# Other places for the modulation units in the first block's weight ring

## What is computed

```python
mod = (c_act @ w_ada + b_ada)[:, None, :]
sh1, sc1, g1, sh2, sc2, g2 = jnp.split(mod, 6, axis=-1)
h = rmsnorm(x, norm1_w) * (1 + sc1) + sh1
u = h @ w_in                       # 1024 x 5632
...                                # pooling, short convolution, 8 attention heads
x = x + g1 * (merged @ w_out)
h2 = rmsnorm(x, norm2_w) * (1 + sc2) + sh2
x = x + g2 * ((jax.nn.silu(h2 @ w_gate) * (h2 @ w_up)) @ w_down)   # D_FF = 2816
```

## Time and profile before

| | us |
|---|---|
| median of 3 runs | 1804.53 (1804.48 to 1804.78) |
| the profiled execution | 1801.64 |
| its span, first to last instruction | 1799.8 |
| first block, first layer: product(0) to product(0) of the second | 51.4 to 509.2 |
| first block, second layer: to the end of product(65) | 509.2 to 928.2 |

### The profile page before, as it was taken

How to read it: one execution, slowest core, us unless ns; L and a number is a source line. 1 busy time by engine, 2 the same in 40 slices (tenths; PEclk the granted TensorE clock), 3 DMA queues, 4 the chain that set the end, 5 groups by cost and what they waited for, 6 DMA issues and landing times.

```text
span 1799.8 us, 18780 instructions
## 1 busy us (share of the span) xinstructions
PE 1572.9 (87%) x7463; PEld 1082.9 (60%) x7463; DVE 924.3 (51%) x1334; ACT 619.3 (34%) x877; POOL 49.8 (3%) x66
## 2 busy tenths in 40 slices
PE   2889987999979998799969995999996996799985
PEld 2667766878767776688858874333335875433331
DVE  4897576864479656654547765110006675311102
ACT  2335544343343454443425651111114572211111
POOL 2000000000000000000020200000000010000000
PEclk9999998999989999899989997999998988899998
DMA  9676445866568634474546324999994416599994
GB/s 341 219 273 215 141 140 173 302 215 210 176 223 282 200 137 151 153 233 146 214 125 204 129 90 192 384 409 409 409 388 150 157 48 241 197 409 409 409 409 190
DMA packets 149963, 427.65 MB, mean 238 GB/s; under 512 B 8104, under 2 KB 16544, under 8 KB 149872
## 3 DMA queue, kind: packets, MB, share of 16 engines
q1 hardware_dynamic: 146192, 417.43, 63.3%
q0 software_dynamic: 3456, 8.87, 1.8%
q10 hardware_dynamic: 224, 0.07, 0.0%
HBM read 425.30 MB, written 1.05 MB: 237 GB/s over the span
## 4 chain that ended last, share of the span: by engine, by line
PE 44%; DVE 6%; SPq 6%; DMA 3%; ACT 1%; issue 1%; DVEq 0%
PE gp L2080 12%; PE gp L2433 9%; PE gp L2252 8%; SPq L725 6%; PE gp L2452 4%; PE mp L2473 2%; DMA raw_more<-in_exp_w_up 2%; PE gp L2418 2%; PE mp L2307 1%; PE mp L2306 1%; PE mp L2271 1%; DVE stats L1623 1%; PE mp L2295 1%; PE mp L2315 1%; DMA raw<-in_w_in 1%
## 5 line engine op out<-in xcount | busy, mean ns | idle before, releaser
L1276 DVE TENSOR_TENSOR wlo<-raw,whi 128x2048 fp32r<-128x2048 f32 (+1 forms) x132 | 289.5, 2194 | 228.8 <-ACT whi L833 227.6
L833 ACT ACTIVATE whi<-raw 128x2048 fp32r<-128x2048 f32 (+1 forms) x132 | 242.2, 1835 | 368.0 <-PE gp L2080 215.7
L2080 PE MATMUL gp<-whi,xt_hi 128*128 128x512 f32 (+1 forms) x800 | 318.6, 398 | 32.1 <-DVE xt_lo L1325 14.1
L2080 PE MATMUL gp<-wlo,xt_hi 128*128 128x512 f32 (+1 forms) x800 | 312.1, 390 | 0.0
L2080 PE MATMUL gp<-whi,xt_lo 128*128 128x512 f32 (+1 forms) x800 | 311.5, 389 | 0.0
L2080 PEld LDWEIGHTS gp<-whi,xt_hi 128*128 128x128 f32 x800 | 154.8, 193 | 73.1 <-DVE wlo L1276 18.1
L2080 PEld LDWEIGHTS gp<-whi,xt_lo 128*128 128x128 f32 x800 | 154.9, 194 | 31.4
L2080 PEld LDWEIGHTS gp<-wlo,xt_hi 128*128 128x128 f32 x800 | 155.1, 194 | 29.1 <-issue 0.2
L1948 DVE TENSOR_SCALAR pr<-slots,key,dg 128x128 f32<-128x128 f32 x64 | 19.3, 344 | 260.5 <-PE gp L2463 260.5
L2252 PE MATMUL gp<-whi,xt_hi 128*128 128x512 f32 (+1 forms) x224 | 85.6, 382 | 6.3 <-DVE xt_lo L1668 3.1
L1186 DVE SCALAR_TENSOR_TENSOR acc<-raw,cact,acc 128x1024 f32<-128x1024 f32 x69 | 88.4, 1282 | 1.4
(11 more groups left out here) (392 smaller groups left out, 2324.6 us busy)
## 6 DMA issues: line engine op xcount, KB each, us to landing
raw<-in_w_in SPq DMA_DIRECT2D x60, 1024.0 KB, 5.9
raw<-in_w_ada SPq DMA_DIRECT2D x42, 1024.0 KB, 5.3
raw_deep<-in_exp_w_down SPq DMA_DIRECT2D x36, 1024.0 KB, 16.9
raw_deep<-in_exp_w_gate SPq DMA_DIRECT2D x30, 1024.0 KB, 14.3
raw_deep<-in_exp_w_up SPq DMA_DIRECT2D x30, 1024.0 KB, 16.7
raw<-in_w_gate SPq DMA_DIRECT2D x20, 1024.0 KB, 5.2
raw<-in_w_up SPq DMA_DIRECT2D x20, 1024.0 KB, 5.3
raw<-in_w_down SPq DMA_DIRECT2D x20, 1024.0 KB, 5.0
```

Source lines behind the costliest of these rows:

```text
L833: act.activation(slot(whi, s % SPLIT, units, cols), slot(raw, g % RAW, units, cols), ACT.Copy).then_inc(hi_done.sem, 1)
L1276: dve.tensor_tensor(slot(wlo, s % SPLIT, units, cols), slot(raw, g % RAW, units, cols), slot(whi, s % SPLIT, units, cols).bitcast(F32), AL ...
L2080: mm = pe.matmul(gp[:, q % 2, t, 0:wide], a[:, chunk, ts], w[:, unit, c0:c0 + wide], start=first and n == 0 and m == 0, stop=last and n == ...
```

## The change

The table that places the modulation units becomes three lists. Units 9 to 11 (vector 2) stand behind split units 2 to 4 as before. Units 12 to 19 (vectors 3 and 4), which stood behind 5 to 12, now stand behind 10, 12, 13, 15, 16, 17, 21 and 22. Units 20 to 31, which stood behind 13 and 32 to 42, stand behind every second unit from 32 to 54. The last stays behind 60.

With that the places of three sums move. TensorE's `sum_mod(3)` goes from behind product(9) to behind the heads, just ahead of `sum_mod(4)`, and VectorE's `take_mod(3)` with it. TensorE's `sum_mod(5)` goes from behind product(35) to behind product(43) and the turning of columns there, and VectorE's `take_mod(5)` from step 37 to step 45. Vectors 3 and 4 now share bank 0 of `mp`, in different columns.

```diff
-LATE = 2
-AFTER = {LATE + s: AHEAD + s for s in range(12)}
-AFTER.update({S_FF + LATE + i: AHEAD + 12 + i for i in range(6 * ADA - 1 - 12)})
-AFTER[S_DOWN + 6] = 6 * ADA + AHEAD - 1
+GATE_AT = (2, 3, 4)
+NORM_AT = (10, 12, 13, 15, 16, 17, 21, 22)
+FF_AT = tuple(S_FF + 2 + 2 * i for i in range(12))
+AFTER = {s: AHEAD + i for i, s in enumerate(GATE_AT + NORM_AT + FF_AT + (S_DOWN + 6,))}
...
-        MOD_BANK = (0, 1, 0, 2, 0, 2)
+        MOD_BANK = (0, 1, 0, 0, 0, 2)
+        MOD_COL = (0, 0, 0, 0, KD, 0)
...
                 for s in range(10):
-                    if s == 9:
-                        take_mod(3)
                     split(s + 2)
...
+                dve.wait_ge(*acc_read.at(l, 5))
+                take_mod(3)
                 take_mod(4)
                 norm_columns(1, 3)
...
-                    if s == S_FF + 7:
+                    if s == S_FF + 15:
                         take_mod(5)
...
-                sum_mod(3, l)
...
-                        pe.wait_ge(*mod_taken.at(l, 4))
+                        pe.wait_ge(*mod_taken.at(l, 3))
...
                 pe.wait_ge(*s_max.at(l, HEADS))
+                sum_mod(3, l)
                 sum_mod(4, l)
...
-                    if s == S_FF + 5:
-                        sum_mod(5, l)
                     if r == 1 and j >= 1:
-                        if j == 2:
+                        if j == 4:
                             pe.wait_ge(*mod_taken.at(l, 6))
                         turn_ab(j - 1)
+                    if s == S_FF + 13:
+                        pe.wait_ge(*ft_lo.at(l, X_ACT + 4))
+                        sum_mod(5, l)
```

More of the change, by code:

```diff
@@ L71 @@
 AHEAD = 2 * ADA + 1
[L72 to L76 removed]
+GATE_AT = (2, 3, 4)
+NORM_AT = (10, 12, 13, 15, 16, 17, 21, 22)
+FF_AT = tuple(S_FF + 2 + 2 * i for i in range(12))
+AFTER = {s: AHEAD + i for i, s in enumerate(GATE_AT + NORM_AT + FF_AT + (S_DOWN + 6,))}
+assert AHEAD % RAW == 0 and max(AFTER) == S_DOWN + 6 and len(AFTER) == 6 * ADA and max(FF_AT) == S_DOWN
 def ring_order():
@@ L1295, in take_mod @@
                     else:
-                        src = gp[:, 0, vec, 0:KD] if l == 0 and vec < 2 else mp[:, MOD_BANK[vec], 0:KD]
+                        c = MOD_COL[vec]
+                        src = gp[:, 0, vec, 0:KD] if l == 0 and vec < 2 else mp[:, MOD_BANK[vec], c:c + KD]
                         dve.tensor_tensor(modc[:, vec, :], src, pcol[:, l, KD * vec:KD * (vec + 1)], ALU.add).then_inc(mod_taken.sem, 1)
@@ L2057, in sum_mod @@
                     bank = gp[:, 0, vec, :] if l == 0 and vec < 2 else mp[:, MOD_BANK[vec % 6], :]
+                    c0 = MOD_COL[vec % 6]
                     for c in range(KD):
-                        mm = pe.matmul(bank[:, c:c + 1], a[:, P * c:P * (c + 1)], ones[:, 0:1], start=True, stop=True)
+                        mm = pe.matmul(bank[:, c0 + c:c0 + c + 1], a[:, P * c:P * (c + 1)], ones[:, 0:1], start=True, stop=True)
                 mm.then_inc(acc_read.sem, 1)
```

1 line of the change is left out of this document (removed).

## The result

| | before | after |
|---|---|---|
| median, same chip | 1804.51 us (8 runs, 1799.58 to 1806.70) | 1811.45 us (8 runs, 1805.44 to 1814.96) |
| ratio, 95% interval | 1 | 1.0049 [1.0033, 1.0065] |
| the profiled execution | 1801.64 | 1805.44 |
| its span, mean granted clock | 1799.8, 0.947 | 1803.6, 0.939 |

The change makes the kernel about 7 us slower. The forecast was 1805.9 us; the time lies in its range of 1797 to 1814, 5.5 us above the forecast. Of the three outcomes that the prediction weighed, "no change within 3.6 us" had the largest chance (47%) and did not come; "slower", which came, had 36%. In the two profiled executions the difference is 3.8 us, where +1.4 was forecast. The profile after was taken of the fastest of its eight runs.

The account below looks back on a forecast made before the run. VectorE was taken to bound the beginning, and a closed ScalarE-VectorE chain, as long as TensorE's step, the heads. First layer -4.6, second +2.6, clock +3.4 gave +1.4 us: median 1805.9 from 1804.5, range 1797 to 1814 (8 in 10).

Parts of the forecast that it names:

- 1 beginning: Products 5 to 9: five units leave, TensorE no longer waits for VectorE; gains 10.3 us first layer, 4.7 second.
- 2 steps 10 to 13: Products 10 to 13: waits left by units behind 11 to 13 vanish; gains 1.7 us first layer, 2.6 second.
- 3 products 14 to 17: Heads: units between split and `soft_max` lengthen the ScalarE-VectorE chain, walked turn by turn; loses 3.8 us each layer.
- 4 products 20 and 21: End of heads: units in steps 9 and 10 plus `sum_mod(3)` on the path; loses 5.2 us each layer.
- 5 products 30 to 43: Feed-forward: spread units let the ring keep up; gains 5.1 us in the first layer, nothing in the second.
- 6 products 50 to 54: End of feed-forward: late units 30 and 31 delay product(54); loses 3.5 us first layer, 0.9 second.
- 7 clock: Whole kernel: of about eleven new or longer waits, two slow products that count; +3.4 us, between 0 and 10.
- C: Beginning: VectorE's norm and rotation of q and k bind steps 5 to 8; +7.5 us, 1813; 9%.
- D: Beginning: loads set the pace, not the units, so part 1's 15.0 us stay away; about 1821 us; 2%.
- Rival A: Heads: `pt` has more lead than walked and units are hidden; 1787.9 us; 10%, and 7% for something between.
- rival B: All eleven new waits: the clock falls behind each, 18.7 us in place of 3.4; 1821.2 us; 8%.
- half of it: New waits: slow clock behind half of them, the half form of the clock rival; 1813 us; 10%.

Follow-up runs that it names:

- second trace of before: The kernel before, run again unaltered for a second trace: 1801.76 us (8 runs).
- with the waits filled: Changed kernel, with TensorE making unread matmuls ahead of `weigh` in head steps 5, 6, 7 and 10 of both layers: 1812.20 us, ratio to before 1.0054.
- heads without: Changed kernel, units behind 15, 16, 17, 21 and 22 loaded but not multiplied, the others there behind `soft_max`: 1789.19 us, ratio to before 0.9918.
- behind `soft_max`: Changed kernel, with VectorE's modulation unit in the head steps moved behind `soft_max`: 1796.71 us, ratio to before 0.9981.
- first group: First of three sets of runs, each on its own chip with the kernel before beside it; median of before here 1801.24 us (32 runs).
- second trace of after: The changed kernel, run again unaltered for a second trace: 1811.90 us (9 runs), ratio to before 1.0054.
- with that time filled: Changed kernel, with 15 unread matmuls filling TensorE's wait ahead of product(54) in the first layer: 1808.92 us, ratio to before 1.0031.
- both mendings: Changed kernel, head-step units behind `soft_max`, and twelve feed-forward units behind two of every three splits, 32 to 48: 1790.69 us, ratio to before 0.9930.

## Why the prediction was right, and where it was off

Counted in the first pair of traces, step by step as it was put, gains negative:

| step | forecast, layers | found, layers |
|---|---|---|
| 1 beginning | -10.3, -4.7 | -10.3, -4.7 |
| 2 steps 10 to 13 | -1.7, -2.6 | -1.6, -2.5 |
| 3 products 14 to 17 | +3.8, +3.8 | +4.3, +5.4 |
| 4 products 20 and 21 | +5.2, +5.2 | +5.8, +5.2 |
| 5 products 30 to 43 | -5.1, 0 | -5.4, -0.3 |
| 6 products 50 to 54 | +3.5, +0.9 | +6.6, +1.2 |
| the other stretches | 0, 0 | -1.2, +2.1 |
| 7 clock | +3.4 together | in the rows above |
| sum | -4.6, +2.6, with the clock +1.4 | -1.8, +6.4, together +4.6 |

The paths and the waits were named rightly, and the forecast's own range, 1800 to 1812, holds the 1811.45 only just: parts 3, 4 and 6 came out dearer than put, most of it through the clock (part 7).

*1 and 2* held to 0.1 us, by the rule of counting products at their full-speed 5.43 us where TensorE will have no wait. Rivals C and D are out with it. Rows 2 themselves were one sample: the second trace of before has 36.8 us, not 33.7, in the second layer, and 86.4, not 88.5, for products 30 to 43.

*3.* The mechanism was right: `weigh` waits for `pt`, `pt` for `soft_max`, `soft_max` for the unit ahead of it. The size is 4.3 at full clock (35.9 with the waits filled, for 31.6), forecast 3.8. The walk gave the waits of the first to the fourth `weigh` as none, 1.2, 2.5 and 2.2. In the trace the second of `weigh`'s lines starts at

```profile
146.74 0.39 PE L2142 MATMUL mp<-u,pt 128*128 128x64 f32 x2
155.68 0.39 PE L2142 MATMUL mp<-u,pt 128*128 128x64 f32 x2
165.67 0.39 PE L2142 MATMUL mp<-u,pt 128*128 128x64 f32 x2
175.22 0.39 PE L2142 MATMUL mp<-u,pt 128*128 128x64 f32 x2
```

and less the 7.49 us of a step without a wait these are 1.45, 2.50 and 2.06 us later each time (a slow product takes part of the 2.50). The missing 0.5 us is the floor: four steps without a wait take 29.9 us, as "heads without" shows, and the walk's waits stood on 29.5. Rival A (idle time hides the units) is out: 9.98 us a turn.

*4* held in these two traces: `sum_mod(3)` 1.85 for 1.8, the two units 4.0 in the first layer (23.9 for 19.9 behind `soft_max`) for 3.5. The same heads took up to 26.6 us in other traces, where the sums and what follows them ran at the lower clock; the forecast has nothing for that.

*5 and 6* is where the forecast went off first. The wait ahead of product(54) was found as forecast, 3.55 us for "about 3.5", with the cause that was named. What the sum left out is that the product behind it then takes 8.3 us: another 2.9 us, in all five traces that have the wait unfilled and all units multiplied. For -5.1 and +3.5 the first layer has -5.4 and +6.6.

*7.* The clock had been given two slow products and 3.4 us for the whole kernel. In the trace of after, product(54) alone uses up 2.9; products 14 to 17 of the second layer lose 1.0 (36.9 for 35.9), product(22) there 1.5. That is 5.4 us, and in the second trace of after the first layer's product(22) (1.7) and products 14 to 17 (1.1) come on top. Not all of it need be the change's: the second trace of before has the second layer's product(22) slow too, 9.05 us for 7.6. Products 18 and 19 of the first layer, 1.5 us slower than the 15.0 in both traces of before, give some back. So the term was mis-sized: 3.4 for some 4 to 7 us, with the largest piece at a place where the forecast had looked at the wait and not at what follows it. The reason not to give it more had been that waits in the heads take place where a slow product costs nothing. For the heads that is right in good part (0 to 1.1 us over the 35.9 with the waits filled, in the four cases of the two traces of after); it does not hold where the next stretch has no wait of its own, at product(54) and product(22). The row from which the term was read says less than the prediction took from it. The stretch with 0.91 is 0.8 us longer than the one with 1.00 (18.8 for 18.0) and not 1.7, and its only idle time, 0.84 us ahead of product(22), comes behind the slow matmuls: there the clock fell behind the sum, not behind a wait.

By the Trainium skill (TensorE: Matmul & The Clock Gate, section "HAM oscillation — how this bites in real kernels") short groups of matmuls with waits between them can start slow each time. This was rival B, and for the longest wait of the change the traces agree each time: 0.64 in product(54) behind 3.55 us of idle time, 1.00 with that time filled. For the waits of about 0.8 us ahead of the second layer's product(54) they don't: 5.9 us. B in full would have been 1821; half of it, 1813, is nearest to what was measured, and had been given 10%.

*From one execution to the median.* The forecast took one difference for both. In the profiled executions it is 3.8 us, between the medians 6.9, and 10.7 on the chip of the first group (1811.90 for 1801.24). The pair in the profiles was a low draw: over the two traces of each kernel the span grows by 6.4 us on average (1799.8 and 1798.5 to 1803.6 and 1807.5), of it 5.2 in the first block, 0.7 in what follows it and 0.5 ahead of product(0). The second block's code is the same, yet it has two lengths. Its opening (500 matmuls), before and after:

```profile
928.20:1037.10 108.90, 94.32 (x500) 78.64 (x500) 80.09 (x163) 57.18 (x110) 24.32 (x30) 0.91 0.49 151
```

```profile
933.10:1044.20 111.10, 96.74 (x501) 80.69 (x501) 80.11 (x163) 56.95 (x110) 24.32 (x30) 0.88 0.49 149
```

It takes 108.9 us in both traces of before, 111.1 in both of after: 2.2 us, and the clock is 0.88 for 0.91. Of the 13 traces, 111 us stand in six of the seven traces with units behind every second feed-forward product (not in "heads without"), and in one of the other six ("both mendings"). The whole of what follows the first block is 872.8 us on average in the seven and 869.8 in the six, but in the pair of the profiles it is shorter after the change (870.4 for 871.5), so the 2.2 us can't simply be added to the first block's. Why the end of the first block should set the clock in the next isn't shown; it stays open, and the count doesn't rule out chance.
